# One inference step of a hybrid decoder trunk: the first layer norm split over two engines, the gate kept by channel, and new orders of work between and behind the expert products

## The chip, the cores and the metric

The kernel runs on one core of a Trainium2 chip. The time is the device time of one execution, in microseconds (us). The engines are PE (TensorE), DVE (VectorE), ACT (ScalarE), POOL (GpSimd) and SP, which here only issues DMAs. Each runs its own list of instructions in order; they meet at semaphores.

## What is computed

272 prompt tokens (16 learned ones ahead of 256) and 32 sample tokens (8 sequences of 4), 304 in all, pass through one layer of width 1024:

```python
x = layer_norm(concat(meta, x_prompt)), layer_norm(x_sample)     # ln_emb
q, fpre, vin, gate, u = split(x @ w_in + b_in)                    # five groups of 512
o = hgrn2(q, (1-lb)*sigmoid(-fpre), vin, log f)                   # 4 heads of 128
o_hg = o * rsqrt(mean(o*o) + eps) * hg_norm_g * silu(gate)
y = s5_scan(u, ...)                                               # complex diagonal scan
z = gelu(y);  o_ssm = z * sigmoid(z @ w_glu + b_glu)
x = layer_norm(ALPHA * x + concat(o_hg, o_ssm) @ w_out)           # ln1
# PEER: 8 heads, 128 x 128 product keys, top 16 of each side, then top 16
a = gelu(u_tab[e] . x);  ffn = sum(softmax(score) * a * v_tab[e])
x = layer_norm(ALPHA * x + ffn)                                   # ln2
```

The states after the last token are outputs too.

## The kernel before

All work is written out by hand, one block per engine. The 304 tokens lie in three tiles (128, 128, 48). The stages follow each other:

- First layer norm (`layer_norm`, L1067 to L1085, on DVE): statistics (L1073, L1076, L1077), subtract the mean and multiply by the gain row (L1081), ACT's square root (`deviation`, L868), reciprocal, then scale and add the bias row (L1084). The gain and bias rows are in `rows_emb`, broadcast to all partitions. PE transposes each tile (`xT`, L497), ACT copies the transposed halves into `x_t` (L885).
- Projections with fp32 matmuls: `u`, `f`, `q` in channel layout (L521; channels on partitions, 304 tokens in the row), `v` and `gate` in token layout (`project_tok`, L525 to L539). A group's weights are 2 MB in a ring of two (`load_w`, L402 to L407); group n waits for the last product of group n - 2. After `u`, SP moves u by 16 small DMAs into `u4` (L421).
- S5: DVE and POOL build its constants from `cols` and `s5raw`. POOL then makes `rot`, a chain of many small instructions that ends in `rot_ready`. PE makes `toep` and X (L578). DVE runs the scan (from L1176), after X and rot, and then reads v.
- HGRN2 in levels h = 0, 1, 2, 4, ..., 64: per level DVE makes `q_dec` (L1263), POOL `k_dec` (L1588), PE the products (L596), DVE picks them through a mask (L1229) and updates `suf` (L1273) and `pre` (L1276). Between the levels (`BETWEEN`) PE puts three gate products and then three S5 outputs `y`; DVE reads them (L1248, L1252). POOL multiplies each gate tile by its sigmoid and by the norm's gain (L1594, L1595).
- ACT runs gelu on y (L946), then makes nine masked copies of v (`v_mask`, L951). Behind them come o (L962), the transposed keys (L969), and the state products S (L679) and Sb (L684). POOL scales the sample states (L1614), DVE adds to them (L1307).
- glu; DVE scales `o_tok` and multiplies by the gate (L1313, L1315); PE transposes it (`oT`), ACT copies it (L983), PE multiplies by `w_out` (`mix`, L712, L719); second layer norm; transposes.
- PEER. Blocks of 512 KB come in by DMA. ACT rounds each half to its high part (`high_part`, L876), POOL subtracts to get the low part (L1620), PE makes three fp32r products for one fp32 one: queries (L738), expert products with u (L738; the last 48 blocks with the gate units between them, L808 and L794), and then the products with v (L835), 24 matmuls a block, which sum in 8 PSUM banks over 128 blocks. Their moving operand is `store` split into `w_hi` (ACT, L1046 and L1041) and `w_lo` (DVE, L1477, L1490, L1495), two buffers each. x1 is put together again (L1484) in eight pieces in the first v blocks.
- The ending: DVE adds the scaled x1 to the sums (L1500), PE transposes (L855), DVE makes statistics (L1507) and subtracts and multiplies (L1513), ACT scales (L1061), POOL adds the bias (L1630); for the last tile DVE does it (L1521).

The order on every engine is the order in the source. `computed` waits for a PE product, `evacuated` for its read, `link` for the instruction itself.

## Time and profile before

| | |
|---|---|
| median of 3 runs | 1229.93 us (1229.81 to 1230.38) |
| the profiled execution | 1228.41 us, its span 1226.6 us |
| instructions | 25373 |
| PE busy | 1167.3 us, 95% of the span |
| POOL busy | 848.5 us, 69% |
| DVE busy | 778.3 us, 63% |
| ACT busy | 549.3 us, 45% |
| mean granted clock of PE | 0.982 |

A row of a timeline gives the start and the duration in us (for merged instructions, of all of them), the engine, the line, the operation with what it writes and reads, how many were merged, and in brackets how long the engine had been idle and who released it. The chain that ended last is followed back from the last instruction, at each step to what released it. A granted clock of 1.00 is 2.4 GHz.

### The profile page before, as it was taken

To read this page: it belongs to the slowest core of one execution; us is meant where nothing else is said; L and a number is where in the kernel's file an instruction comes from. 1 tells how busy PE (TensorE), PEld (TensorE's weight loads), DVE (VectorE), ACT (ScalarE), POOL (GpSimd) and SP (SyncE) were. 2 spreads that over 40 slices of the span, in tenths; PEclk is the share of its full clock that TensorE was granted. 3 is DMA by queue.
4 is the path that set the end of the run, shared out by engine and by line. 5 is a ranking of instruction groups with operands and counts; after the bars stand their busy time and mean duration, and the time that the engine had idled before them with its cause. 6 is when DMAs were issued, how large, how long until landed. Compare 5 with 4: busy or idle time off the path is not lost.

```text
span 1226.6 us, 25373 instructions
## 1 busy us (share of the span) xinstructions
PE 1167.3 (95%) x8561; PEld 1103.2 (90%) x8561; DVE 778.3 (63%) x1645; ACT 549.3 (45%) x987; POOL 848.5 (69%) x745
## 2 busy tenths in 40 slices
PE   4999969989999999999999999989999999999995
PEld 3685767469899999999999999989999999999995
DVE  6908976339999999432899999953333333333336
ACT  2240132035576676776333333345554554554553
POOL 4991673056688988887555555578888888888884
PEclk9999978989999999999999999999999999999998
DMA  7331143243344445444333333344544544544442
GB/s 269 119 109 69 70 111 86 78 161 132 121 160 165 165 160 171 163 162 157 133 106 118 120 117 111 115 135 158 169 166 160 170 163 162 171 161 164 171 158 86
DMA packets 63623, 173.06 MB, mean 141 GB/s; under 512 B 9872, under 2 KB 19216, under 8 KB 63456
## 3 DMA queue, kind: packets, MB, share of 16 engines
q1 hardware_dynamic: 63584, 172.58, 42.1%
q8 instruction: 20, 0.33, 0.1%
q14 instruction: 19, 0.16, 0.0%
HBM read 167.62 MB, written 3.69 MB: 140 GB/s over the span
## 4 chain that ended last, share of the span: by engine, by line
PE 85%; DVE 9%; issue 2%; DMA 1%; SPq 1%; POOL 1%; ACT 0%; DVEq 0%; ACTq 0%; POOLq 0%
PE bank L835 33%; PE bank L738 25%; PE bank L808 13%; PE bank L794 5%; PE bank L521 3%; PE bank L712 2%; DVE q_dec L1263 2%; PE bank L694 1%; PE bank L756 1%; DVE pre L1276 1%; SPq L421 1%; DVE att L1229 1%; POOL s_samp L1614 1%; DMA w_ring<-in_w_in 1%; PE bank L563 1%
## 5 line engine op out<-in xcount | busy, mean ns | idle before, releaser
L1620 POOL TENSOR_TENSOR parts<-raw,parts 128x512 fp32r<-128x512 f32 x544 | 718.2, 1326 | 288.7 <-ACT parts L876 287.6
L876 ACT ACTIVATE parts<-raw 128x512 fp32r<-128x512 f32 x544 | 343.5, 632 | 456.9 <-PE bank L835 202.8
L835 PE MATMUL bank<-w_hi,parts 128*128 128x288 f32 x2048 | 407.6, 295 | 3.6 <-DVE w_lo L1477 2.4
L835 PEld LDWEIGHTS bank<-w_hi,parts 128*128 128x128 f32 x2048 | 327.7, 188 | 4.1 <-DVE w_lo L1477 2.6
L738 PE MATMUL bank<-xw,parts 128*128 128x288 f32 x2304 | 310.6, 296 | 2.1 <-DVE xw L1333 1.1
L738 PEld LDWEIGHTS bank<-xw,parts 128*128 128x128 f32 x2304 | 309.2, 189 | 3.2 <-issue 3.1
L835 PE MATMUL bank<-w_lo,parts 128*128 128x288 f32 x1024 | 301.5, 294 | 0.0
L1495 DVE TENSOR_TENSOR w_lo<-store,w_hi 128x288 fp32r<-128x288 f32 x122 | 147.7, 1211 | 241.5 <-ACT w_hi L1041 241.5
L835 PEld LDWEIGHTS bank<-w_lo,parts 128*128 128x128 f32 x1024 | 192.0, 188 | 0.0
L808 PE MATMUL bank<-xw,parts 128*128 128x288 f32 x1152 | 171.2, 300 | 0.0
L808 PEld LDWEIGHTS bank<-xw,parts 128*128 128x128 f32 x1152 | 156.1, 188 | 0.0
L1432 DVE TENSOR_SCALAR hot<-bank,idx_t 128x128 f32<-128x128 f32 x288 | 97.8, 401 | 0.0
L794 PE MATMUL bank<-hot 128*128 128x128 f32 x576 | 76.0, 275 | 0.0
L794 PEld LDWEIGHTS bank<-hot 128*128 128x128 f32 x576 | 71.2, 191 | 0.1
L1441 DVE TENSOR_TENSOR store<-store,bank 128x512 f32<-128x512 f32 x72 | 49.5, 688 | 24.0 <-issue 9.3
L521 PE MATMUL bank<-x_t,w_ring 128*128 128x304 f32 x192 | 53.3, 442 | 3.5 <-DMA w_ring<-in_w_in 2.9
L521 PEld LDWEIGHTS bank<-x_t,w_ring 128*128 128x128 f32 x192 | 38.5, 202 | 17.9 <-DMA w_ring<-in_w_in 3.4
L1041 ACT ACTIVATE w_hi<-store 128x288 fp32r (+1 forms) x126 | 53.9, 428 | 0.0
L1427 DVE TENSOR_TENSOR hot<-bank,idx_t 128x512 f32<-128x512 f32 x72 | 49.2, 683 | 0.2 <-DVE store L1421 0.2
L1391 DVE TENSOR_TENSOR tk_eq<-tk_eq,tk_idxf 128x512 f32<-128x512 f32 (+1 forms) x24 | 35.1, 1502 | 0.4
L1588 POOL TENSOR_TENSOR k_dec<-k_t,suf 128x512 f32<-128x512 f32 (+1 forms) x18 | 27.8, 1567 | 10.0 <-DVE suf L1273 7.6
L1357 DVE MAX8 tk_val<-scores 128x8 f32<-128x128 f32 (+1 forms) x96 | 20.9, 277 | 20.4 <-ACT scores L1003 19.6
(295 smaller groups left out, 1027.3 us busy)
## 6 DMA issues: line engine op xcount, KB each, us to landing
raw<-in_blocks SPq DMA_DIRECT2D x272, 512.0 KB, 3.2
w_ring<-in_w_in SPq DMA_DIRECT2D x5, 2048.0 KB, 8.6
w_ring<-in_w_out SPq DMA_DIRECT2D x2, 2048.0 KB, 7.8
s_samp<-in_state SPq DMA_DIRECT2D x8, 256.0 KB, 5.9
rows_ln<-in_rows SPq DMA_DIRECT2D x4, 512.0 KB, 5.0
out_hg_sample<-s_samp SPq DMA_DIRECT2D x8, 256.0 KB, 5.1
rows_emb<-in_rows SPq DMA_DIRECT2D x2, 512.0 KB, 6.1
wglu<-in_w_glu SPq DMA_DIRECT2D x1, 1024.0 KB, 5.3
```

Of the source, the lines that this page charges most:

```text
L521: last = mm(b[:, 0:NT], w[:, c, m * P:(m + 1) * P], x_t[:, c, :], start=c == 0, stop=c == DC - 1)
L738: last = mm(b[:, 0:NP], w[:, a, :], xw[:, x, c, :], start=(c == 0 and (a, x) == (0, 0)), stop=(c == DC - 1 and a == 1))
L794: last = mm(b[:, v * P:(v + 1) * P], hot[:, u % 2, 0, v, :], hot[:, u % 2, 1, v, :], start=True, stop=True)
L808: last = mm(bank[s][:, 0:NP], w[:, a, :], xw[:, x, c, :], start=(c == 0 and (a, x) == (0, 0)), stop=(c == DC - 1 and a == 1))
L835: last = mm(v_bank(c)[:, 0:NP], vv, w[:, s, :], start=first and (a, w) == (0, w_hi), stop=False, skip_group_check=True)
L876: A(parts[:, q % 4, 0, :], raw[:, s % 4, (q % 2) * 512:(q % 2 + 1) * 512], ACT.Copy).then_inc(hi_ready, 1)
L1041: A(w_hi[:, s % 2, :], store[:, bass.ds(4 * i + s, 1), :].squeeze(1), ACT.Copy).then_inc(whi_ready, 1)
L1427: V.tensor_tensor(hot[:, k % 2, 0, :, :], wide_lanes, idx_t[:, 0, UNIT * k:UNIT * k + UNIT].unsqueeze(2).broadcast_to([P, UNIT, P]), ALU.i ...
L1432: last = V.tensor_scalar(hot[:, k % 2, 1, v, :], lanes, idx_t[:, 1, t:t + 1], idx_t[:, 2, t:t + 1], ALU.is_equal, ALU.mult)
L1441: V.tensor_tensor(st, st, bank[4 + k % 3][:, :].rearrange("p (t j) -> p j t", j=NK), ALU.mult).then_inc(gate_scaled, 1)
L1495: V.tensor_tensor(w_lo[:, s, :], store[:, bass.ds(2 * i + s, 1), :].squeeze(1), w_hi[:, s, :].bitcast(F32), ALU.subtract).then_inc(wlo_rea ...
L1620: G.tensor_tensor(parts[:, q % 4, 1, :], raw[:, q // 2 % 4, (q % 2) * 512:(q % 2 + 1) * 512], parts[:, q % 4, 0, :].bitcast(F32), ALU.subt ...
```

## The change

- **First layer norm.** DVE makes only the statistics (`embed_stats`) and the shift -mean * rstd (`embed_shift`). ACT normalizes a tile in one pass (`normalize`). Gain and bias are by channel (`embt`) and go on where the transposed tile is read: half of the channels by ACT (`read_x`), half by DVE. The residual needs the same in token layout; DVE multiplies x_tok by the gain row and adds the bias row later, behind the memset of `suf`.
- **DMA order.** `rows_emb` goes behind the first two weight groups, `cols` and `s5raw` behind the first; the third weight group is issued ahead of the u4 moves; `wglu` and the states no longer wait for POOL's gate.
- **Gate.** Four products in channel layout. ACT makes the sigmoid from the bank, DVE adds the bias and multiplies by the sigmoid, POOL multiplies by the norm's gain. DVE applies it where it reads the transposed o (`oT`), which ACT did before. The y parts come one level later.
- **Between the u and the v products.** ACT makes the first two `w_hi` ahead of its last gelu; DVE makes the x1_t pieces one at a time, each followed by one `w_lo`.
- **Ending.** The last two v blocks go by halves, with the transposes of the first half ahead of the last half product; the last block's `w` has its own buffer (`w_end`). DVE makes the first half's statistics between the two halves of y_t.

```diff
-            for i in range(2):
-                sp.dma_start(rows_emb[:, i, :], rows_in[i, :].partition_broadcast(P)).then_inc(rows_sem, 16)
...
-            sp.dma_start(cols[:, :], cols_in).then_inc(cols_sem, 16)
-            sp.dma_start(s5raw[:, :, :, :].rearrange("p a b c -> p (a b c)"), s5bc).then_inc(cols_sem, 16)
...
+            sp.dma_start(ident[:, :], consts_in[:, 0:P]).then_inc(ident_sem, 16)
+            sp.dma_start(embt[:, :], cols_in[:, NCOLS:NCOLS + 2 * DC]).then_inc(embt_sem, 16)
...
             load_w(0)
+            sp.dma_start(cols[:, :], cols_in[:, 0:NCOLS]).then_inc(cols_sem, 16)
+            sp.dma_start(s5raw[:, :, :, :].rearrange("p a b c -> p (a b c)"), s5bc).then_inc(cols_sem, 16)
+            load_w(1)
...
+            for i in range(2):
+                sp.dma_start(rows_emb[:, i, :], rows_in[i, :].partition_broadcast(P)).then_inc(rows_sem, 16)
...
+            load_w(2)
             for m in range(4):
                 evacuated(sp, "u", m)
             for j in range(SC):
                 for q in range(4):
                     sp.dma_start(u4[32 * j:32 * j + 32, :, :].rearrange("p (m q) n -> p m q n", q=4)[:, :, q, :],
                                  u_chan[32 * q:32 * q + 32, :, j, :]).then_inc(u4_moved, 16)
-            for n in range(2, 7):
+            for n in range(3, 7):
                 load_w(n)
...
-            sp.wait_ge(gate_done, 3)
+            evacuated(sp, "v", 2)
...
-            v_block(NK // 2 - 1, 0)
-            v_block(NK // 2 - 1, 1, final=True)
...
+            def last_product(s, h):
+
+                pe.wait_ge(wlo_ready, NK - 1 + s)
+                pe.wait_ge(lo_ready, 8 * ROUNDS - 3 + 2 * s + h)
+                hi, lo = (w_end[:, 0, :], w_end[:, 1, :]) if s else (w_hi[:, 0, :], w_lo[:, 0, :])
+                for c in range(4 * h, 4 * h + 4):
+                    for (a, w) in ((0, hi), (0, lo), (1, hi)):
+                        vv = parts[:, 2 * s + h, a, (c % 4) * P:(c % 4 + 1) * P]
+                        last = mm(v_bank(c)[:, 0:NP], vv, w, start=False, stop=False, skip_group_check=True)
+                    if s:
+                        last.then_inc(y_full, 1)
...
+            last_product(0, 0)
+            last_product(1, 0)
+            last_product(0, 1)
+            y_transposes(0)
+            last_product(1, 1)
+            y_transposes(1)
...
+            def normalize(t):
+
+                n = TILES[t][1]
+                act.wait_ge(shift_ready, t + 1)
+                A(x_tok[:n, t, :], x_tok[:n, t, :], ACT.Identity, bias=shift[:n, t:t + 1],
+                  scale=rstd[:n, 3 + t:4 + t]).then_inc(x0_ready, 1)
+
+            def read_x(t):
+
+                t0, n = TILES[t]
+                computed(act, "xT", t, 0)
+                for c in range(4):
+                    last = A(x_t[:, c, t0:t0 + n], bank_of("xT", t, 0)[:, c * n:(c + 1) * n], ACT.Identity,
+                             bias=embt[:, DC + c:DC + c + 1], scale=embt[:, c:c + 1])
+                readout(last, "xT", t, 0)
+
             deviation(0, 0)
-            for t, (t0, n) in enumerate(TILES):
-                if t < 2:
-                    deviation(0, t + 1)
-                for i in range(2):
-                    computed(act, "xT", t, i)
-                    readout(A(x_t[:, 4 * i:4 * i + 4, t0:t0 + n],
-                              bank_of("xT", t, i)[:, 0:4 * n].rearrange("p (c n) -> p c n", n=n), ACT.Copy),
-                            "xT", t, i)
+            deviation(0, 1)
+            normalize(0)
+            deviation(0, 2)
+            normalize(1)
+            act.wait_ge(embt_sem, 16)
+            read_x(0)
+            normalize(2)
+            read_x(1)
+            read_x(2)
...
+            for m in range(HEADS):
+                computed(act, "gate", m)
+                A(gate_sig[:, m, :], bank_of("gate", m)[:, 0:NT], ACT.Sigmoid, bias=gcol[:, m:m + 1]).then_inc(gate_s, 1)
...
-            for t, (t0, n) in enumerate(TILES):
-                computed(act, "oT", t)
-                readout(A(ohg_t[:, :, t0:t0 + n], bank_of("oT", t)[:, 0:4 * n].rearrange("p (h n) -> p h n", n=n),
-                          ACT.Copy), "oT", t)
...
             act.wait_ge(gate_scaled, 3 + LATE_TURNS * UNITS)
             for s in range(2):
                 A(w_hi[:, s, :], store[:, s, :], ACT.Copy).then_inc(whi_ready, 1)
+            late_gelus(V_ROUND - 1, [3])
...
-            for s in range(2, 4):
-                high_part(ROUNDS - 1, 2 * s)
-                high_part(ROUNDS - 1, 2 * s + 1)
-                w_high(NK // 4 - 1, s)
+            high_part(ROUNDS - 1, 4)
+            high_part(ROUNDS - 1, 5)
+            w_high(NK // 4 - 1, 2)
+            A(w_end[:, 0, :], store[:, NK - 1, :], ACT.Copy).then_inc(whi_ready, 1)
+            high_part(ROUNDS - 1, 6)
+            high_part(ROUNDS - 1, 7)
...
-                layer_norm(t, rows_emb, 0, rows_sem, x0_ready)
...
+            def embed_shift(t):
+
+                n = TILES[t][1]
+                dve.wait_ge(ln_std, t + 1)
+                link(V.reciprocal(rstd[:n, 3 + t:4 + t], rstd[:n, 3 + t:4 + t]))
+                V.tensor_scalar(shift[:n, t:t + 1], mv[:n, 2 * t:2 * t + 1], rstd[:n, 3 + t:4 + t], -1.0,
+                                ALU.mult, ALU.mult).then_inc(shift_ready, 1)
+
+            embed_stats(0)
+            embed_stats(1)
+            embed_shift(0)
+            embed_stats(2)
+            embed_shift(1)
+            embed_shift(2)
+            dve.wait_ge(embt_sem, 16)
+            for t, (t0, n) in enumerate(TILES):
+                computed(dve, "xT", t, 1)
+                for c in range(4):
+                    last = V.tensor_scalar(x_t[:, 4 + c, t0:t0 + n], bank_of("xT", t, 1)[:, c * n:(c + 1) * n],
+                                           embt[:, 4 + c:5 + c], embt[:, DC + 4 + c:DC + 5 + c], ALU.mult, ALU.add)
+                readout(last, "xT", t, 1)
...
+            dve.wait_ge(rows_sem, 32)
+            for t, (t0, n) in enumerate(TILES):
+                x = x_tok[:n, t, :]
+                link(V.tensor_tensor(x, x, rows_emb[:n, 0, :], ALU.mult))
+                link(V.tensor_tensor(x, x, rows_emb[:n, 1, :], ALU.add))
...
+                    dve.wait_ge(gate_s, k + 1)
+                    last = V.scalar_tensor_tensor(gate[:, k, :], b[:, 0:NT], gcol[:, k:k + 1], gate_sig[:, k, :],
+                                                  ALU.add, ALU.mult)
...
-                V.tensor_tensor(o_tok[:n, t, :], o_tok[:n, t, :], gate[:n, t, :], ALU.mult).then_inc(og_ready, 1)
+                V.tensor_tensor(ot, ot, rms[:n, 4 * t:4 * t + 4].unsqueeze(2).broadcast_to([n, HEADS, P]),
+                                ALU.mult).then_inc(og_ready, 1)
...
+            dve.wait_ge(gate_done, HEADS)
+            for t, (t0, n) in enumerate(TILES):
+                computed(dve, "oT", t)
+                readout(V.tensor_tensor(ohg_t[:, :, t0:t0 + n],
+                                        bank_of("oT", t)[:, 0:4 * n].rearrange("p (h n) -> p h n", n=n),
+                                        gate[:, :, t0:t0 + n], ALU.mult), "oT", t)
...
             for c in range(DC):
                 V.tensor_tensor(x1_t[:, c, :], xw[:, 0, c, :].bitcast(F32), xw[:, 1, c, :].bitcast(F32),
                                 ALU.add).then_inc(x1t_ready, 1)
-                if c % 4 == 3:
-                    for s in range(2):
-                        dve.wait_ge(whi_ready, 2 * (c // 4) + s + 3)
-                        j = 2 * (c // 4) + s + 2
-                        V.tensor_tensor(w_lo[:, s, :], store[:, j, :], w_hi[:, s, :].bitcast(F32),
-                                        ALU.subtract).then_inc(wlo_ready, 1)
-            with V.Fori(3, NK // 2, 1) as i:
-                for s in range(2):
+                dve.wait_ge(whi_ready, c + 3)
+                V.tensor_tensor(w_lo[:, c % 2, :], store[:, c + 2, :], w_hi[:, c % 2, :].bitcast(F32),
+                                ALU.subtract).then_inc(wlo_ready, 1)
...
+            for i in range(2):
+                for c in range(4 * i, 4 * i + 4):
+                    dve.wait_ge(y_full, c + 1)
+                    V.scalar_tensor_tensor(y_t[:, c, :], x1_t[:, c, :], ALPHA, v_bank(c)[:, 0:NP],
+                                           ALU.mult, ALU.add).then_inc(yT_ready, 1)
+                if i == 0:
+                    for t in range(3):
+                        half_stats(t, 0)
...
+                link(half_stats(t, 1))
...
-                if h >= 16:
-                    t = {16: 0, 32: 1, 64: 2}[h]
-                    n = TILES[t][1]
-                    pool.wait_ge(gate_s, t + 1)
-                    link(G.tensor_tensor(gate[:n, t, :], gate[:n, t, :], gate_sig[:n, t, :], ALU.mult))
-                    G.tensor_tensor(gate[:n, t, :], gate[:n, t, :], rows_v[:n, 2, :], ALU.mult).then_inc(gate_done, 1)
+                if h >= 8:
+                    m = {8: 0, 16: 1, 32: 2, 64: 3}[h]
+                    evacuated(pool, "gate", m)
+                    G.tensor_scalar(gate[:, m, :], gate[:, m, :], gcol[:, HEADS + m:HEADS + m + 1], None,
+                                    ALU.mult).then_inc(gate_done, 1)
```

## Rows read from the trace of the kernel before

**Rows 1.** The page's part 4: the chain that ended last, shares by engine.

```profile
PE 85%; DVE 9%; issue 2%; DMA 1%; SPq 1%; POOL 1%; ACT 0%; DVEq 0%; ACTq 0%; POOLq 0%
```

**Rows 2.** Timeline: start, duration (us), engine, line, form, idle before; 0 to 45.

```profile
4.79 1.29 DVE L1073 BATCH_NORM_STATS2 small<-x_tok 128x6 f32<-128x512 f32 x2 [3.90 <-DMA x_tok<-in_x_prompt]
...
8.72 1.28 DVE L1081 SCALAR_TENSOR_TENSOR x_tok<-x_tok,small,rows_emb 128x1024 f32<-128x1024 f32 x1 [2.21 <-DMA rows_emb<-in_rows]
...
14.42 3.67 PE L497 MATMUL bank<-ident,x_tok 128*128 128x128 f32 x16 [14.42 <-DMA lane<-in_consts]
```

**Rows 3.** The chain that ended last in order: start, duration, what; 0 to 78.

```profile
21.91 18.62 PE bank L521 x64
...
51.75 7.97 DMA w_ring<-in_w_in
...
59.77 18.33 PE bank L521 x64
```

**Rows 4.** Stretches: busy by engine (count), granted clock, DMA share, GB/s.

```profile
40.50:56.90 16.40, 16.39 (x65) 11.82 (x63) 16.05 (x27) 3.43 (x7) 15.80 (x21) 1.00 0.41 117
...
59.80:64.00 4.20, 4.20 (x10) 2.92 (x11) 2.76 (x5) 0.00 (x0) 3.81 (x16) 0.59 1.05 392
```

**Rows 5.** Timeline, 45 to 125.

```profile
60.73 0.79 DVE L1161 COPY pre<-f_t 128x1216 f32<-128x1216 f32 x1
...
60.75 0.86 POOL L348 TENSOR_TENSOR rot<-pool_tmp 128x16 f32<-128x16 f32 x1
...
92.21 0.22 POOL L348 TENSOR_TENSOR pool_tmp<-pool_tmp 128x16 f32<-128x16 f32 x1
...
96.76 1.29 DVE L1176 TENSOR_TENSOR cm_scan<-x_s,rot 128x1088 f32<-128x1088 f32 x1 [33.96 <-ACT x_s L937]
```

**Rows 6.** Timeline of the gated-attention levels, 125 to 178.

```profile
136.73 0.69 DVE L1248 TENSOR_TENSOR gate<-bank,rows_v 128x512 f32<-128x512 f32 x1
...
155.17 2.01 POOL L1595 TENSOR_TENSOR gate<-gate,rows_v 128x512 f32<-128x512 f32 x1
...
156.09 1.65 DVE L1276 TENSOR_TENSOR pre<-pre 128x512 f32<-128x512 f32 x1
...
165.48 5.61 ACT L951 ACTIVATE v_mask<-v_tok,lane 48x512 f32<-48x512 f32 x9
...
169.80 4.08 DVE L1276 TENSOR_TENSOR pre<-pre 128x512 f32<-128x512 f32 x1
```

**Rows 7.** Timeline of the states and of the mix, 178 to 260.

```profile
179.31 1.17 PE L679 MATMUL bank<-v_tok,k_end 128*128 128x128 f32 x8
...
190.57 9.43 POOL L1614 TENSOR_TENSOR s_samp<-s_samp,pre 128x512 f32<-128x512 f32 x8 [13.12 <-PE bank L668]
...
212.72 1.31 ACT L983 ACTIVATE ohg_t<-bank 128x512 f32<-128x512 f32 x3
...
213.64 3.67 PE L712 MATMUL bank<-w_ring,ohg_t 128*128 128x512 f32 x8
```

**Rows 8.** Timeline between the expert stages, 796 to 817.

```profile
796.51 0.69 DVE L1441 TENSOR_TENSOR store<-store,bank 128x512 f32<-128x512 f32 x1 [0.15 <-PE bank L794]
...
800.91 0.75 ACT L1046 ACTIVATE w_hi<-store 128x288 fp32r<-128x288 f32 x2
...
802.38 0.40 PE L835 MATMUL bank<-w_hi,parts 128*128 128x288 f32 x1 [2.38 <-DVE w_lo L1477]
...
811.29 4.84 DVE L1484 TENSOR_TENSOR x_t<-xw 128x288 f32<-128x288 f32 x4
...
816.63 0.40 PE L835 MATMUL bank<-w_hi,parts 128*128 128x288 f32 x1 [1.27 <-DVE w_lo L1490]
```

**Rows 9.** Timeline of the ending, from 1208.

```profile
1213.07 1.29 DVE L1507 BATCH_NORM_STATS2 small<-bank 128x6 f32<-128x512 f32 x2 [1.36 <-PE bank L855]
...
1216.34 1.15 ACT L1061 ACTIVATE y_tok<-y_tok,small 128x1024 f32<-128x1024 f32 x1 [1.31 <-DVE small L1518]
...
1224.15 0.34 SPq L478 DMA_DIRECT2D out_y_sample<-y_tok  x1
```

More of the change, by code:

```diff
@@ L513, in weights, with project_part @@
                 return w_ring[:, n % 2, :, :]
+            def project_part(kind, m):
+                w = weights(W_GROUP[kind])
+                b = begin(kind, m)
+                for c in range(DC):
+                    last = mm(b[:, 0:NT], w[:, c, m * P:(m + 1) * P], x_t[:, c, :],
+                              start=c == 0, stop=c == DC - 1)
+                last.then_inc(ps_full, 1)
             def project(kind):
[L517 removed]
                 for m in range(4):
[L519 to L523 removed]
+                    project_part(kind, m)
             def project_tok(kind, t):
@@ L1030, in _, with late_gelus @@
                 u_blocks(i)
-            with act.Fori(U_ROUND + EARLY // 4, V_ROUND, 1) as i:
-                for s in range(4):
+            def late_gelus(i, slots):
+                for s in slots:
                     high_part(i, 2 * s + 4)
```

129 lines of the change are left out of this document (67 added, 62 removed).

## The prediction

> **What bounds the kernel now.** Read the chain of work that ended last first: TensorE carries 85% of it and the vector engine 9% [rows 1]. So an edit is worth time where the chain is not on TensorE, or where TensorE waits. Five such places are touched. (1) The start: the first layer norm waits 2.21 us for its gain and bias rows and then passes over each tile twice [rows 2]; TensorE starts the projections at 21.91, waits until 59.77 for the third group of weights, and needs 18.33 us for the third group against 16.4 for the second [rows 3, 4]. (2) From 96.76 the chain is on the vector engine (the S5 scan, then the gated-attention levels), whose first instruction there had waited 33.96 us [rows 5]. (3) The levels and the state products behind them [rows 6, 7]. (4) Two waits between and in the expert stages, 2.38 and 1.27 us [rows 8]. (5) The ending after the last product [rows 9]. Everything between these is TensorE back to back and is not changed.
>
> **The start.** x_tok's first tile is there at 4.79 [rows 2]. The rows are no longer ahead of tile 1: 1 MB less in the queue, so I take tile 1 at 6.8 (estimate: 0.5 MB behind a tile that landed at 4.79, at the 392 GB/s that the queue moves in the last row of [rows 4]). Statistics cost 1.29 for two halves [the same form in rows 2, 9] plus some 0.35 for the two small instructions behind them (estimate), so tile 0's end at 6.4, tile 1's at 8.5, the shift at 8.8. ACT then normalizes a tile in 1.15, the price of its 128x1024 pass with a scale [rows 9]: tile 0 10.0, tile 1 12.0, and, behind four reads of tile 0, tile 2 14.2. TensorE's transposes take 1.8 per tile at the rate of the row of 14.42 (16 in 3.67 [rows 2]). The bank reads become four of 128x128 per half tile: at least 0.5 (one wide read, a third of the 1.31 in [rows 7] and a little more), at most 4 x 0.69 (four of the wide bank read of DVE [rows 6]); I take 1.1 on ACT and 1.4 on DVE, between them, since each is a quarter as wide. The last ends at 16.4. Weights group 0 has 1.3 MB ahead of it instead of 3.1 and lands near 13 (estimate by the same rate), so it doesn't bind. The u projection starts at 16.5 instead of 21.91: -5.4, between -4 and -6. Next, group 2's load is issued ahead of the 16 small u4 moves instead of behind them. It can go when u is done (35.1), needs the 7.97 of [rows 3] and is there at 43; f ends at 51.5. The wait (56.9 to 59.8) goes, and with it the slow first stretch of q: the granted clock was 0.59 for 4.2 us after that wait, towards the lower of the two levels (1.2 GHz), and q took 18.33 where f took 16.4. So q ends at 67.8 instead of 78.1, -10.3, and X, behind it on TensorE and read by ACT, 10.3 earlier as well: about 86.0.
>
> What is late next? The scan also waits for rot, a chain of small GpSimd instructions that ends at 92.43 [rows 5]. It hangs on the S5 constants, which ACT and DVE begin after the x reads: it moves by only -5.5, to 86.9. And the change puts six new vector instructions beside it: x_tok times gain, plus bias, for three tiles, directly behind the suf memset, at about 55 to 64, with both inputs in SBUF. Each is nearly the 128x1088 form of 1.29 [rows 5]: 1.2, so 7.3 together. They fall on the middle of GpSimd's chain. Rows 5 show what that does: while DVE copied 128x1216 for 0.79 us, GpSimd's 16-column instruction lasted 0.86 against 0.22 for its like at 92.21, so about 0.64 of 0.79 was lost. At that share (0.8) six cost 0.8 x 7.3 = 5.9, at full 7.3, at none 0; I take 6.2, a little over the share because these instructions have two SBUF inputs, while the copy had one. Rot is then ready at 93.1 and the scan starts there: **-3.6** instead of the -10 that TensorE won. Bounds -9.9 (no loss) and -2.5.
>
> The Trainium skill (SBUF — State Buffer, "Who interferes with whom") says that a vector instruction with two SBUF inputs and a GpSimd instruction that reads SBUF exclude each other for the whole instruction. By that rule alone the loss would be 7.3 and the sum 1.1 us later than mine, 1219.9; it speaks against this placement.
>
> ACT's Identity behind Sqrt does not occur in this trace; if it needed its own table the start would pay some table loads, which the rot bound would hand on. The Trainium skill (ScalarE: Activation LUTs, "Table sets: the hidden batching unit") puts identity into every set, so no load; this leaves the sum unchanged.
>
> **The levels and the states.** These are vector-bound, one level in 6.85 us (half of 156.09 to 169.80, [rows 6]). The gate is read in four channel tiles of 304 columns by one instruction instead of 512-column adds at 0.69 [rows 6]: about 0.43 each (scaled), against 0.69 twice and 0.85: -0.5. Its new wait is for ACT's sigmoid of the same bank, done about 0.5 after TensorE's product, 4.1 us of work begun a level earlier; ahead of the wait nothing else is due, behind it are q_dec and TensorE's next products. I cost it at nothing; cover 3 us. GpSimd's two 128x512 products per tile (1.7 to 2.0) leave, and one scaling of 304 columns per head comes (about 1.0). That is worth more on the vector engine than on GpSimd: the pre update of 128x512 took 1.65 beside such a product and 4.08 at the last level, queued behind the product and two of GpSimd's own k_dec [rows 6], where 512 columns alone should take about 0.68 (1.29 for 1088 columns, [rows 5]). With GpSimd idle when suf is ready, pre goes first: -0.95 twice and -3.4 once. The last level ends near -5.8 + 0.5 for the y part that now comes after it: y2 moved one level later, because four gates stand ahead of the y parts. Here the gain meets a new bound: ACT can start y2's gelu only then (pre ends at 167.6 on the old clock, read and gelu 0.5 each, estimated from the 0.69 row: 168.6), and v_mask, 5.61 for nine [rows 6], now follows at 168.6 to 174.2 instead of 165.48 to 171.1. Behind v_mask stand on ACT the read of o and of the first kend, 0.5 to 0.6 each (two of the wide copies in the 1.31 of [rows 7]); the first state product starts at 175.4 instead of 179.31: **-3.9**, between -2 (a late y2 product) and -5.3 (ACT not binding). From there the chain is as now: states, the second and third o, GpSimd's s_samp (9.43 from 190.57 [rows 7]), glu. The weight load for glu, the state loads and the 16 z moves on SP no longer stand behind the gate product on GpSimd; they are hidden already and gain nothing. keysT goes behind the outputs, 60 us before its use.
>
> The gate now multiplies in channel layout on the read of oT, on DVE instead of ACT. The vector engine saves three products, hidden by its wait for ACT's last glu sigmoid. But its 0.69 read can start only behind the last ossm product (about 213.53), where ACT's copy of 212.72 ran beside it and TensorE went on at 213.64 [rows 7]: 214.3, **+0.65**, between 0 and 0.8.
>
> **The seam.** TensorE waits 2.38 before 802.38 for w_lo, which came behind ACT's last gelu: w_hi started at 800.91 [rows 8]. The gate scaling on which w_hi depends is done at 797.2 (0.69 from 796.51, [rows 8]), so in the new order w_hi is made near 797.8 to 798.5 and w_lo near 799.3; the ACT work pushed back (two high parts, the last gelu) moves by 0.1, and the vector engine's last two late products are due only at the seventh and eighth bank of the block, 2.4 us in. Gain 2.38. The second wait, 1.27 before 816.63, is that of four x1_t sums in one piece, 4.84 under GpSimd's products, ahead of w_lo [rows 8]; one at a time (1.2) plus a w_lo (1.3) is 2.5 per block of 3.2. Gain 1.27. **-3.65**, between -2.4 and -3.7.
>
> **The ending.** Twelve transposes (1.4) go ahead of the last half product, so that ends 1.4 later. DVE has read half 0 of three tiles by then, but these three 0.65 push the last y_t to about 1213.5, transposes to 1214.1, and statistics start at 1214.2 instead of 1213.07. Each of the three tiles then takes 0.65 less than the 3.15 of now (1213.07 to 1216.34 less ACT's start [rows 9]): +1.1 - 1.95 = -0.8 for the sample tile, whose store is issued at 1224.15; the second prompt tile, through ACT and GpSimd, gains only some 0.2. **-0.6**, between +0.5 and -1.3.
>
> **Sum.** -3.6 - 3.9 + 0.65 - 3.65 - 0.6 = -11.1. The profiled execution took 1228.41 with a span of 1226.6, and the median is 1229.93, 0.12% off; so the span would be 1215.5, and the median **1218.8**.
>
> **Rivals.** (A) GpSimd's chain is not slowed, or only little: the scan starts at 86.9 and the whole start gain comes, 1212.5. For it: GpSimd's instructions are short and have their own overhead to hide in. Against it: the 0.86 row. Chance 0.2, with what lies between (1213 to 1216) 0.1 more. (B) The attention gain is swallowed, since y2's product or ACT's v_mask comes later than I think, or the seam keeps its wait because w_lo meets GpSimd's product: each alone costs 3.65 to 3.9, 1222.5 to 1222.7. For it: y2 is a chain of three engines in the one place where all are busy. Chance 0.12. (C) Slower than before: TensorE idles some 10 us before level 1, since its projections are early and the scan is not, and stays at the lower clock in the levels. There 24 products of 128x128 at 0.229 and 16 of 304 columns at 0.51 (twice 16.4/64) make 13.7 a level against the vector engine's 6.85, so 6.85 lost a level; it decides against the change from two whole levels (13.7), and four give 1246. Against it: after the wait before 59.77 the clock was back within 4.2 us of matmuls [rows 4]. Chance 0.03. (D) The change doesn't do what it says, each place being hidden by another: within 0.2%, chance 0.02; against it, five separate waits.
>
> **How the numbers follow.** The forecast and its neighbours from 1216 to 1222 hold 0.53, A with its partial form 0.3, B 0.12, C 0.03, D 0.02. The range reaches from 1211.5, A with a little more at the end, to 1223, B: about 0.85. 0.2% (2.5 us) is what a measurement can tell from no change. Faster 0.95, same 0.02, slower 0.03.
>
> **What would show it.** Profile after: first projection near 16.5 with no wait at the third group; the last rot instruction at about 93 and the scan's first instruction released by GpSimd, not by ACT's X read (A: near 87, released by either); the last pre update at 0.7; v_mask starting right after a gelu, with ACT not idle ahead of kend; no wait over 0.3 on TensorE between 795 and the end. Wrong if rot's end moves with the u projection, if a level lasts over 7 us, or if TensorE waits for the banks that DVE's late products free.

## The result and the profile after

The changed kernel takes 1224.09 us in the median of five executions (1220.96 to 1224.97) against 1229.93: a ratio of 0.9953, 95% interval 0.9940 to 0.9965, 5.8 us faster. In a second comparison the same two took 1221.14 and 1228.9 (0.9936, 0.9919 to 0.9952), 7.8 us. The ratios are formed on their own and differ a little from those of the medians; where two comparisons are set against each other below, both are given. 1218.8 had been forecast, 11.1 faster. The profiled execution took 1220.96, with a span of 1219.2 against 1226.6: 7.4 less. So two things are to be explained: 3.7 us missing from the profiled execution, and up to 4 us by which other executions of the changed kernel are longer than the profiled one.

The chain that ended last, shares by engine: less of it is on the vector engine than in [rows 1].

```profile
PE 90%; DVE 5%; issue 2%; POOL 1%; ACT 1%; DMA 0%; SPq 0%; DVEq 0%; POOLq 0%
```

The start answers [rows 2, 3, 5]. Columns of a timeline as there; 4 to 95 us, and the chain's piece of the projections first.

```profile
17.14 51.86 PE bank L530 x192
```

```profile
4.91 1.29 DVE L1139 BATCH_NORM_STATS2 small<-x_tok 128x6 f32<-128x512 f32 x2 [4.04 <-DMA x_tok<-in_x_prompt]
...
9.99 3.79 PE L507 MATMUL bank<-ident,x_tok 128*128 128x128 f32 x16 [9.99 <-ACT x_tok L909]
...
57.96 1.23 DVE L1243 TENSOR_TENSOR x_tok<-x_tok,rows_emb 128x1024 f32<-128x1024 f32 x1
...
58.13 1.16 POOL L354 TENSOR_TENSOR pool_tmp<-rot,pool_tmp 128x32 f32<-128x32 f32 x1
59.25 1.30 POOL L355 TENSOR_TENSOR pool_tmp<-rot,pool_tmp 128x32 f32<-128x32 f32 x1
...
77.53 0.25 POOL L354 TENSOR_TENSOR pool_tmp<-rot,pool_tmp 128x32 f32<-128x32 f32 x1
...
86.59 0.74 ACT L980 ACTIVATE x_s<-bank 128x456 f32<-128x456 f32 x2 [0.79 <-PE bank L591]
...
93.44 0.22 POOL L359 TENSOR_TENSOR pool_tmp<-pool_tmp 128x16 f32<-128x16 f32 x1
...
94.04 1.29 DVE L1257 TENSOR_TENSOR cm_scan<-x_s,rot 128x1088 f32<-128x1088 f32 x1 [28.58 <-PE bank L552]
```

The projections run in one piece from 17.14 (21.91 before), without the wait for the third group, and end at 69.00 instead of 78.10. The scan starts only 2.7 us earlier, and what it waits for has changed. Before, rot was complete at 92.43 and the scan stood 4.3 us behind it, released by ScalarE's read of X ([rows 5]). Now ScalarE has read X at 87.33, and the scan begins 0.4 us behind GpSimd's last rot instruction (93.44 plus 0.22); the profile's naming of TensorE as the releaser doesn't fit these times.

The levels and the states, ScalarE's and TensorE's rows; they answer [rows 6, 7]. Here o(t) is the attention output of tile t, and the state product is the first of S, the prompt's state.

```profile
166.28 0.46 ACT L990 ACTIVATE z<-z 128x304 f32<-128x304 f32 x1 [5.18 <-DVE z L1329]
166.64 5.61 ACT L995 ACTIVATE v_mask<-v_tok,lane 48x512 f32<-48x512 f32 x9
172.16 0.57 ACT L1006 ACTIVATE o_tok<-bank 128x512 f32<-128x512 f32 x1
172.63 1.54 ACT L1013 ACTIVATE k_end<-bank 128x512 f32<-128x512 f32 x3
173.26 2.08 PE L692 MATMUL bank<-v_tok,k_end 128*128 128x128 f32 x8 [2.67 <-ACT k_end L1013]
...
176.73 0.63 PE L669 MATMUL bank<-s_prompt,q_dec 128*128 128x128 f32 x2
...
181.79 0.42 PE L675 MATMUL bank<-v_tok,att 48*48 48x128 f32 x4 [1.26 <-issue]
...
186.87 9.43 POOL L1709 TENSOR_TENSOR s_samp<-s_samp,pre 128x512 f32<-128x512 f32 x8 [15.68 <-PE bank L681]
```

The same place in the kernel before: a pair of o(1), the start of o(2), and then two stretches behind 178: busy time by engine, granted clock, DMA share, GB/s.

```profile
181.61 0.39 PE L656 MATMUL bank<-s_prompt,q_dec 128*128 128x128 f32 x2
...
185.49 0.42 PE L662 MATMUL bank<-v_tok,att 48*48 48x128 f32 x4 [1.26 <-issue]
```

```profile
178.00:180.00 2.00, 2.00 (x14) 1.80 (x13) 0.00 (x0) 1.55 (x3) 0.00 (x0) 0.61 1.22 290
180.00:182.00 2.00, 1.17 (x11) 1.01 (x10) 0.69 (x1) 0.15 (x1) 0.00 (x0) 1.00 1.21 290
```

v_mask follows its gelu at once, as forecast, and the first state product waits for what ScalarE does behind it. This product starts 6.05 us earlier than in [rows 7], but its eight parts take 2.08 instead of 1.17, and the pairs of o(1) 0.63 instead of 0.39. o(2) starts at 181.79 instead of 185.49, only 3.70 earlier; GpSimd's s_samp, behind o(2), also starts 3.70 earlier: 1.0 more than the scan gave.

The mix and the ending; they answer [rows 7, 9].

```profile
210.42 1.13 PE L725 MATMUL bank<-w_ring,ohg_t 128*128 128x512 f32 x2 [0.64 <-DVE ohg_t L1403]
```

```profile
1206.80 0.70 DVE L1592 BATCH_NORM_STATS2 small<-bank 128x6 f32<-128x512 f32 x1 [0.82 <-PE bank L874]
...
1216.69 0.34 SPq L488 DMA_DIRECT2D out_y_sample<-y_tok  x1
```

Between 780 and the end TensorE now has one wait, where [rows 8] has two (2.38 and 1.27). Waits of TensorE there: line waited for, us in total, times, longest.

```profile
PE bank L874 <- DVE y_t L1597: 1.0, 1, 1.0
```

This wait is new, in the ending, where the transposes of the second half wait for y_t. The forecast's sign of "no wait over 0.3" is not met there, though its own account of the ending has the transposes behind the last y_t.

### The profile page after: what moved, and what is told of

Its sections match the earlier page's. It is cut to its first block, busy times and chain, and to the rows that moved or that the text cites. A ratio compares the mean times of both kernels' runs of the same rounds, so it can differ in the third digit from the quotient of the medians.

```text
span 1219.2 us, 25381 instructions
## 1 busy us (share of the span) xinstructions
PE 1164.7 (96%) x8561; PEld 1104.6 (91%) x8561; DVE 775.2 (64%) x1660; ACT 552.2 (45%) x994; POOL 853.2 (70%) x743
## 4 chain that ended last, share of the span: by engine, by line
PE 90%; DVE 5%; issue 2%; POOL 1%; ACT 1%; DMA 0%; SPq 0%; DVEq 0%; POOLq 0%
PE bank L845 33%; PE bank L751 25%; PE bank L821 13%; PE bank L530 5%; PE bank L807 5%; PE bank L725 2%; PE bank L609 1%; PE bank L707 1%; PE bank L769 1%; POOL s_samp L1709 1%; PE bank L591 1%; PE bank L576 1%; PE bank L732 1%; PE bank L552 1%; DVE q_dec L1340 0%
## 5 line engine op out<-in xcount | busy, mean ns | idle before, releaser
L845 PE MATMUL bank<-w_hi,parts 128*128 128x288 f32 x2016 | 400.8, 295 | 0.0
L845 PEld LDWEIGHTS bank<-w_hi,parts 128*128 128x128 f32 x2016 | 322.6, 188 | 0.0
L845 PE MATMUL bank<-w_lo,parts 128*128 128x288 f32 x1008 | 296.8, 294 | 0.0
L1574 DVE TENSOR_TENSOR w_lo<-store,w_hi 128x288 fp32r<-128x288 f32 x116 | 140.5, 1211 | 228.4 <-ACT w_hi L1084 228.4
L845 PEld LDWEIGHTS bank<-w_lo,parts 128*128 128x128 f32 x1008 | 189.1, 188 | 0.0
L530 PE MATMUL bank<-x_t,w_ring 128*128 128x304 f32 x256 | 69.3, 432 | 1.7 <-ACT x_t L917 1.7
L530 PEld LDWEIGHTS bank<-x_t,w_ring 128*128 128x128 f32 x256 | 49.8, 196 | 19.2 <-issue 3.4
L1438 DVE MAX8 tk_val<-scores 128x8 f32<-128x128 f32 (+1 forms) x96 | 20.9, 277 | 20.2 <-ACT scores L1042 19.4
```

Of the source, the lines that this page charges most:

```text
L530: last = mm(b[:, 0:NT], w[:, c, m * P:(m + 1) * P], x_t[:, c, :], start=c == 0, stop=c == DC - 1)
L845: last = mm(v_bank(c)[:, 0:NP], vv, w[:, s, :], start=first and (a, w) == (0, w_hi), stop=False, skip_group_check=True)
L1574: V.tensor_tensor(w_lo[:, s, :], store[:, bass.ds(2 * i + s, 1), :].squeeze(1), w_hi[:, s, :].bitcast(F32), ALU.subtract).then_inc(wlo_rea ...
```

## The experiments

Two theories and their rivals stand behind them. Clock: TensorE's granted clock falls to the lower level (1.2 GHz) at waits, and behind the levels that takes back what ScalarE's order leaves. Lock: the six vector products on x_tok hold GpSimd up and set the scan. The rivals: the parts themselves brought less, or the experts lost it.

**The changed kernel again.** No edit.

> The changed kernel unchanged, to see where its ordinary run (1224 us, mean granted clock 0.977) differs from the profiled one (1221.0, 0.982). Theory 1, the clock: TensorE idles longer ahead of the first state product than before, and in ordinary runs it spends about 6 us more at the lower level (1.2 GHz) somewhere between the attention levels and the first expert product, which costs about 3 us: 1224 again, and a profile at 0.977 shows such a stretch between 165 and 265 us. Theory 2, the experts: the 3 us sit in the expert stages (more waits, or slower transfers), so the stretch from the first product behind the seam to the end is longer than in the profile at hand, with the granted clock 1.00 there.

Measured: 1221.14 in the median of four (1220.03 to 1225.37); the profiled execution is the long one, 1225.37 with the granted clock at 0.976, 4.4 us above that of the first profile. Its rows:

```profile
7.74 1.29 DVE L1139 BATCH_NORM_STATS2 small<-x_tok 128x6 f32<-128x512 f32 x2 [0.96 <-DMA x_tok<-in_x_prompt]
...
189.31 11.51 PE L697 MATMUL bank<-v_mask,k_end 48*128 48x128 f32 x64
...
200.75 3.91 PE L707 MATMUL bank<-z_t,wglu 128*128 128x304 f32 x7
```

Two stretches of either profile follow, the one at hand first, then that of the first profile: busy time by engine, granted clock, DMA share, GB/s.

```profile
190.00:196.00 6.00, 6.00 (x39) 6.00 (x38) 5.72 (x10) 0.55 (x2) 6.00 (x6) 0.66 0.00 0
196.00:204.00 8.00, 8.00 (x30) 6.76 (x30) 6.02 (x11) 1.46 (x2) 1.91 (x2) 0.50 0.28 80
```

```profile
190.00:196.00 6.00, 6.00 (x42) 6.00 (x42) 4.11 (x7) 1.50 (x2) 6.00 (x5) 0.74 0.00 0
196.00:204.00 8.00, 7.68 (x19) 5.30 (x19) 7.52 (x14) 0.51 (x1) 0.30 (x1) 0.56 0.81 221
```

The 4.4 us come in four pieces, all ahead of 280 us. The second tile of x arrives at 7.74, and the vector engine, in whose row its statistics stand ahead of the first tile's shift, waits 0.96 for it; this reaches the scan (95.25 against 94.04, +1.2). From there to o(2) +0.4. The per-sample state products take 11.51 instead of 9.15, since the stretch at the lower level begins in them earlier and lasts longer, and glu waits for them, not for GpSimd: glu starts at 200.75 against 197.17, another +2.0; from there to the first expert product 0.4 comes back. The first 120 expert products take 18.98 instead of 17.79, +1.2. The experts behind are the same to 0.1 us. So the first theory's place held, and 3.2 of the 4.4 us are of the size that it gave; 1.2 are the load's arrival, which no theory had. Its forecast that the median would be 1224 again did not: three of the four executions took 1220.0 to 1221.3, where four of the first five had taken 1223.8 to 1225.0.

**The new start alone**, on the kernel before:

```diff
-                layer_norm(t, rows_emb, 0, rows_sem, x0_ready)
+            embed_stats(0)
+            embed_stats(1)
+            embed_shift(0)
...
+                link(V.tensor_tensor(x, x, rows_emb[:n, 0, :], ALU.mult))
+                link(V.tensor_tensor(x, x, rows_emb[:n, 1, :], ALU.add))
```

> The kernel before with only the new start: the two-engine layer norm, the new order of the loads, the x_t reads with gain and bias, and the six vector products on x_tok. Nothing of the levels, the seam or the ending. Theory 1: the scan starts 2.7 us earlier and everything behind it too, so 1227.2; in ordinary runs up to 3 us are given back to the clock (1228 to 1230). Rival: additive parts, 1227.2 in every run. If the products on x_tok did not slow GpSimd's chain, the scan would start at about 88 and the time would be near 1221.

Measured: 1226.58 (ten executions, 1225.28 to 1228.28) against 1228.9, ratio 0.9983 (0.9973 to 0.9992): 2.3 us, and the scan at 93.94. That is the rival's case, 2.7 us expected: what the scan gained arrives, and the clock took nothing that can be measured here.

**The new seam and the new ending alone**, on the kernel before:

```diff
+            late_gelus(V_ROUND - 1, [3])
...
-                if c % 4 == 3:
...
+            last_product(0, 1)
+            y_transposes(0)
+            last_product(1, 1)
+            y_transposes(1)
```

> The kernel before with only the new seam and the new ending. Theory 1 (the 3 us that are missing in ordinary runs of the changed kernel are the clock's, ahead of the experts): the whole 4.25 of the profile arrive in every run, 1225.7. Theory 2 (they are lost in the experts): 1227 to 1229.

Measured: 1224.72 (seven executions) against 1228.9, ratio 0.9966 (0.9954 to 0.9977): 4.2 us. Forecast for the two were 3.65 + 0.6. They arrive in full; nothing is missing in the experts.

**The channel-layout gate alone**, on the kernel before (the parts of levels, states and mix):

```diff
-        BETWEEN = {h: job for h, job in zip(LEVELS, [("gate", t) for t in range(3)] + [("y", b) for b in range(3)])}
+        BETWEEN = {h: job for h, job in zip(LEVELS, [("gate", m) for m in range(HEADS)] + [("y", b) for b in range(3)])}
```

> The kernel before with only the channel-layout gate: gate products and reads by channel, the y parts one level later, the gate's multiplication on the read of oT. Nothing of the start, the seam or the ending. Theory 1 (the forecast's step, corrected): the levels end 5.0 earlier, v_mask and the reads behind it let the first state product start 3.3 earlier, TensorE is then at the lower level for S and o(1) and only some 1.0 is left at o(2), and 0.5 goes at the mix: -0.5, between 0 and -1.5, so 1228.4 against 1228.9 for the kernel before. Rival: the step was right and the loss in the profile was chance: -3.25, 1225.6.

Measured: 1231.51 (ten executions, 1226.67 to 1233.11) against 1229.67; the ratio is 1.0007 (0.9995 to 1.0019), no difference that is clear of the noise. By the medians it is 1.8 us slower: four executions took 1226.67 to 1229.67, the other six 1231.19 to 1233.11. The 0.5 us expected are not seen. In its profile the first state product starts 3.4 us earlier (175.91 against 179.31) and again takes 2.08; o(2) is 0.84 earlier and the mix 0.26. So in the profiled execution 0.3 is left of the 3.25 forecast for this part. That profile also shows something new at the seam, whose waits this kernel keeps: behind the same wait of 2.38 the clock falls.

```profile
802.00:806.00 4.00, 3.90 (x21) 3.90 (x22) 2.80 (x8) 0.63 (x1) 1.03 (x1) 0.69 0.42 135
```

In the kernel before that stretch is at 1.00. The first 48 products behind the wait take 8.16 instead of 6.64, so it costs this execution 1.5 us; whether it is what lifts the others was not looked at.

By their ratios the three parts give -2.1 - 4.2 + 0.9 = -5.4 us, by their medians -2.3 - 4.2 + 1.8 = -4.7, against -5.8 and -7.8 measured for all of them. Each part is known to 1.2 to 1.5 us, so they add within the noise; an interplay of up to 2 us is not ruled out.

**Idle products for TensorE ahead of o(0) and of the first state product**, in the changed kernel:

```diff
+                    mm(b[:, 0:P], ident[:, :], v_tok[:, 0, 0:P], start=True, stop=True)
...
+            idle_products(("o", 0), 12)
...
                     k_ends()
+                    idle_products(("S", 0), 14)
```

> The changed kernel with idle work for TensorE: 12 products of 128x128 ahead of o(0) and 14 ahead of the first state product, in banks that the next products overwrite from their start. ScalarE's order stays, so the first state product starts at 173.3 or up to 0.5 later. Theory 1 (the slow stretch behind is the clock's answer to the idle stretch): S, o(1) up to o(2) take 6.1 instead of 8.5 to 9.0 us, and the time falls by 2 to 2.9, 1218.3 to 1219.2 against 1221.2. Rival (the clock falls there for another reason, such as the products of 48 rows or the whole chip's load): 8.5 stay and the time is that of the changed kernel or up to 0.5 more.

Measured: 1219.29, ratio 0.9914 (0.9897 to 0.993) where the changed kernel has 0.9936 in the second comparison: 2.7 us by the ratios, 1.9 by the medians, with intervals that overlap. The trace is clearer. TensorE, from the last idle products on, and the stretch 172 to 180, with the same stretch of the changed kernel below:

```profile
170.81 3.29 PE L657 MATMUL bank<-v_tok,ident 128*128 128x128 f32 x28
173.94 1.06 PE L701 MATMUL bank<-v_tok,k_end 128*128 128x128 f32 x8
...
176.12 0.39 PE L677 MATMUL bank<-s_prompt,q_dec 128*128 128x128 f32 x2
```

```profile
172.00:180.00 8.00, 5.91 (x51) 5.59 (x51) 1.81 (x5) 3.16 (x7) 0.00 (x0) 1.00 0.40 92
```

```profile
172.00:180.00 8.00, 5.91 (x29) 5.64 (x30) 0.69 (x1) 2.50 (x6) 0.00 (x0) 0.57 0.45 93
```

The state product starts 0.7 later, since the idle products overran, and from it to o(2) (180.00) it is 6.06 instead of 8.53 us. Work that computes nothing took the stretch at the lower level away: the clock theory is shown for this stretch. That agrees with the Trainium skill (TensorE: Matmul & The Clock Gate, "Part 1: The HAM clock gate (the "warmup" mystery)"), which says that the array is put to half its clock once it has idled. Both waits, the one ahead of o(0) and the one ahead of the state product, were filled at once, so which of them brings the stretch is not told apart.

**The k_end copies on VectorE instead of ScalarE**, in the changed kernel:

```diff
-                computed(act, "kend", t)
...
+                computed(dve, "kend", t)
+                readout(V.tensor_copy(k_end[:n, t, :, :],
```

> The changed kernel with one move: the three copies of k_end go from ScalarE, where they stand behind the nine v_mask copies (5.61 us), to VectorE, which is idle from 168 to 175. Theory 1 (v_mask is what the first state product waits for, and the idle TensorE then runs at the lower level): the first state product starts at about 170.0 instead of 173.26; the idle stretch before it is 0.5 us instead of 2.67, so S and the first half of o(1) may also go at full rate, 2 us more. Together 3 to 5.5 us less than the changed kernel: 1219 to 1221 against 1224. Rival: the states are bound by the GpSimd chain k_dec, q_mask, s_samp, or by the loads of s_samp, and the gain is under 1 us.

Measured: 1215.91 (1215.67 to 1216.24), ratio 0.9897 (0.9881 to 0.9914): 5.2 us less than the changed kernel beside it (4.8 by the ratios).

```profile
167.10 2.04 PE L667 MATMUL bank<-v_tok,att 128*128 128x128 f32 x8 [2.75 <-DVE att L1311]
...
170.04 1.89 DVE L1360 COPY k_end<-bank 128x512 f32<-128x512 f32 x3 [1.86 <-PE bank L646]
170.89 1.06 PE L692 MATMUL bank<-v_tok,k_end 128*128 128x128 f32 x8
```

The state product starts 2.4 earlier and goes at full rate, as do o(1) and S; o(2) is 4.8 earlier, half of it by the clock. The low level has not gone from here: in this execution it falls on o(0) (2.04 instead of 1.13) and the transposes, where TensorE would wait for GpSimd's k_dec anyway. That may be the execution and not the move, since the changed kernel's long execution has o(0) at 2.05 too.

**The products on x_tok moved to the mix**, in the changed kernel; the load of their two rows moves with them, behind those of the next layer norm:

```diff
-                link(V.tensor_tensor(x, x, rows_emb[:n, 0, :], ALU.mult))
...
+            scale_x(0)
+            scale_x(1)
...
+                    if (t, i) == (0, 1):
+                        scale_x(2)
```

> The changed kernel with the six vector products on x_tok (gain and bias of the first layer norm) moved from beside GpSimd's rot chain to the vector engine's idle time behind the reads of oT, 211 to 224 us, where GpSimd does nothing; their two rows are loaded behind those of the next layer norm. Theory 1 (two busy vector inputs hold GpSimd up): rot's last instruction at 87.3 instead of 93.44, the scan starts at 88.2, released by ScalarE's X read or by GpSimd, 5.9 earlier, and all behind it: 1215.3 against some 1221.2 for the changed kernel. Rival 1 (the six products cost GpSimd little, its chain was only shifted): under 1 us. Rival 2: the chain gains 5.9 at the scan but TensorE's clock or the loads for glu take part of it back: 1217 to 1219.

Measured: 1215.68, ratio 0.9881 (0.9864 to 0.9897), 5.5 us below the changed kernel's 1221.14 (6.8 by the ratios).

```profile
87.44 0.22 POOL L360 TENSOR_TENSOR pool_tmp<-pool_tmp 128x16 f32<-128x16 f32 x1
88.05 1.29 DVE L1252 TENSOR_TENSOR cm_scan<-x_s,rot 128x1088 f32<-128x1088 f32 x1 [30.07 <-POOLq L1675]
```

GpSimd's chain ends 6.00 us earlier with nothing changed in it, and the scan follows. The lock theory is shown, its rival (the chain had only moved) is out; that it is the vector products and not the moved load is seen in the rows at 58.13 and 59.25, where GpSimd's instructions last as long as the vector products beside them.

**Both moves.**

> Both moves together: the products on x_tok behind the reads of oT, and the copies of k_end on VectorE. Theory 1: the two are at different places of the chain and add: 1215.9 - 5.9 = 1210.0, with the first state product at about 165.0 and the second row of o at 171. Rival: the loads that start at a fixed time (the state, the weights for glu, the z moves) become late, and 1 to 3 us stay: 1211 to 1213.

Measured: 1210.96 (1209.72 to 1215.2), ratio 0.9854 (0.9832 to 0.9876); three of the four executions lie at 1211.4 or below. The two add within 0.5 us by the medians and 1.5 by the ratios.

**Idle products ahead of the last transposes of x1**, in the changed kernel, then with both moves:

```diff
+            b = begin("x1T", 2, 0)
+            for _ in range(30):
+                mm(b[:, 0:P], ident[:, :], ident[:, :], start=True, stop=True)
```

> The changed kernel with 30 products of 128x128 for TensorE in its 5.0 us of waiting ahead of the last eight transposes of x1 (before the first expert product), in a bank that these transposes then overwrite. Theory 1 (a stretch at the lower level answers an idle stretch): the low stretch at 250 to 257 us goes, and with it about half its length in time, so 2.5 to 3.0 us: 1218.2 to 1218.7 against 1221.2 for the changed kernel. Rival: the clock is low there for another reason, 1221.2 or up to 0.5 more.

> Both moves (products on x_tok late, k_end copies on VectorE) and the 30 idle products ahead of the last transposes of x1. Theory 1: the three add: 1211.0 - 2.7 = 1208.3. Rival: 1210 to 1211, the low stretch comes all the same.

Measured: 1222.39 (ratio 0.9939) and 1210.79 (0.9849), no gain in either. The stretch went as expected, the size of one term was missed:

```profile
247.70 6.86 PE L742 MATMUL bank<-ident 128*128 128x128 f32 x60
254.50 0.70 PE L507 MATMUL bank<-ident,x_tok 48*128 48x48 f32 x8
256.33 16.22 PE L754 MATMUL bank<-xw,parts 128*128 128x288 f32 x120 [1.13 <-DVE xw L1417]
```

The low stretch at 250 is gone (16.22 for 120 products, 17.79 before). But 30 products take 6.86 us, 0.229 each, in a place of 5.0. The last transposes start at 254.50 instead of 252.00; 0.8 of that stands ahead of the mix already, so TensorE came 1.7 us late, and that is what the clock gave back. With 18 and both moves:

> Both moves and 18 idle products ahead of the last transposes of x1 instead of 30. In the trace of the kernel with 30, they took 6.86 us (0.229 each) in a place of 5.0, so TensorE reached the transposes 2 us late; 18 take 4.1. Theory: the last transposes are at 240.6 again, the low stretch behind them is gone (the first 120 products take 16.2 instead of 18.6), so 2.0 to 2.4 us less than the kernel with both moves: 1208.6 to 1209.0 against 1211.0. Rival: what is left of the idle time (0.9 us, then 1.3) is enough for the clock to fall again: 1211.

Measured: 1209.66 (five executions, 1208.0 to 1211.15), ratio 0.9841 (0.9828 to 0.9855), 19.4 us below the kernel before and the fastest here. The first 120 products take 17.63 (18.61 with both moves alone), not 16.2: a part of the low stretch stays, between 242 and 247, so the gain over both moves is 1.3 us instead of 2.0 to 2.4, and with these spreads not certain.

**The per-sample state products behind glu and the transposes of o**, with both moves and 30 idle products:

```diff
+        JOBS += [("glu", m) for m in range(4)] + [("oT", t) for t in range(3)]
         JOBS += [("Sb", b) for b in range(NB)]
-        JOBS += [("glu", m) for m in range(4)] + [("oT", t) for t in range(3)]
```

The vector engine's sums on s_samp move behind the reads of oT with them.

> As the kernel with both moves and the idle products, and with the eight per-sample state products (9.15 us) behind the glu products and the transposes of o instead of ahead of them, so that glu does not wait for GpSimd's scaling of s_samp. Theory: TensorE is busy from the last state product to the mix without a wait: mix starts at 196.0 instead of 199.0, another 2.5 to 3.3 us, 1205.2 to 1205.8; if the stretch at the lower level between 180 and 191 stays, it now falls on glu or on the per-sample products alike and nothing of it is won. Rival: the vector engine, which has the squares of o, rms, the ossm products, the reads of oT and the eight sums in one row, becomes the bound ahead of the mix, and the time is that of the kernel without this move or 1 to 2 us more.

Measured: 1210.87, ratio 0.9847, the same as without it (1210.79, 0.9849). The mix starts 1.9 us earlier, and then:

```profile
187.63 10.11 PE L710 MATMUL bank<-v_mask,k_end 48*128 48x128 f32 x64
197.67 5.90 PE L725 MATMUL bank<-w_ring,ohg_t 128*128 128x512 f32 x8
```

```profile
176.00:190.00 14.00, 13.33 (x77) 10.53 (x74) 12.18 (x24) 6.55 (x10) 9.88 (x8) 1.00 0.21 70
190.00:202.00 12.00, 12.00 (x50) 9.29 (x50) 9.56 (x14) 0.00 (x0) 0.00 (x0) 0.58 0.29 80
```

Eight products of the mix take 5.90 instead of 3.70. The stretch at the lower level has moved with the per-sample products: they start at 187.63 instead of 177.09, the clock goes down near 192 instead of 181.5, and the rest of the stretch now falls on the mix.

## Why the prediction was right or wrong, point by point

**The start: right in its mechanism, 0.9 us too good.** The projections began at 17.14 instead of the 16.5 of the forecast, since the x_t reads on ScalarE (2.61 for the last eight) took longer than the 1.1 per tile that was chosen, and the S5 constants behind them moved by 4.9 instead of 5.5. The loss of GpSimd was 6.0 where 6.2 had been taken, so rot was complete at 93.66 instead of 93.1; and the scan follows it by 0.4, which the forecast had put at nothing. The table load that it ruled out did not come: ScalarE's loads are at 0.73 and 16.80, none between the square roots and the Identity passes. Rival A is what comes only when the six products stand elsewhere: then the scan starts at 88.05. The rule by which the loss would be 7.3, that of the Trainium skill (SBUF — State Buffer, "Who interferes with whom"), is borne out by the rows, and 7.3 was still not its price: the two engines alternated. Each of six GpSimd instructions lasted as long as one vector product (1.16 to 1.30 beside 1.22 to 1.23; the same form takes 0.25 alone, at 77.53), so from 58.13 to 65.58 GpSimd lost all but the 1.4 us that its own six take without them. The loss falls short of the rule's by what GpSimd did in that time.

**The levels and the states: 2.9 of 3.9 us failed, and this is the step that made the miss.** The mechanism of the levels came as forecast: pre at 0.69 in the last three, the levels 5.0 earlier relative to the scan, v_mask behind the late gelu. One term was too good: the gate's four reads took 0.53 each, 2.1 in all against 2.2 before, a gain of 0.1 and not 0.5; the state product came 3.3 earlier beyond the scan, not 3.9. The other 2.35 us are the step that failed, "From there the chain is as now". TensorE had waited 2.67 us just before the state product (and 2.75 before o(0)), and went at the lower level through S and most of o(1): 8.53 us to o(2) instead of 6.18. The kernel before has its stretch at the lower level too, up to 179.5, but its state product starts at 179.31, at its end, and takes 1.17; the changed kernel's starts inside it. The kernel with idle products and the one with k_end on VectorE both have 6.06 there, and the gate alone, whose first state product again takes 2.08, gives nothing. The forecast knew this mechanism and priced it once, in rival C, for the wrong place: in the levels, where the clock did fall ahead of level 1 (0.62 from 121.6 to 125.5) and cost nothing, since the vector engine goes from one instruction to the next there without a wait. The forecast's sign of a level over 7 us could not tell anything: the first levels last 7.03, 7.02 and 6.88 us, and 7.04, 7.03 and 7.00 in the kernel before. Behind the levels, where TensorE is the chain, it was not asked.

**The mix: 0.5 lost where 0.65 was forecast. The seam: right.** Both waits are gone. **The ending: 0.6 as forecast, but partly by luck.** The statistics start 0.6 us late against the products ahead of them (forecast 1.1), and each of the three tiles takes 0.6 less, as forecast; but the last vector instruction of the sample tile takes 2.15 instead of 1.55, beside GpSimd's addition, which the forecast did not have. The two errors cancel, and the store of the sample tile is 0.6 early.

**The sum.** -2.7 - 1.0 + 0.5 - 3.65 - 0.6 = -7.45, against 7.4 in the profiled execution. **The step from there to the median failed too**: the forecast carried over the 0.12% by which the profiled execution of the kernel before lies under its median. That kernel's 50 executions lie between 1227.3 and 1231.5, the changed kernel's nine between 1220.0 and 1225.4. The one long execution that was profiled shows what can lengthen it: it has the stretches at the lower level longer in the three places behind the levels, and a first layer norm that waits for the second tile's load. That the other long executions are long for the same reason is not shown: their mean clocks are 0.976 to 0.979, but two of the short ones have 0.979 as well. What decides in which execution the stretches are long was not found. Nor is it settled why the first comparison gave 5.8 and the second 7.8; their intervals overlap.

## What to carry to other kernels

When a part ahead of TensorE gets shorter and another engine's row doesn't, ask what TensorE does in the gap and what it runs just behind it: here a wait of 2.7 us in front of dependent products was followed by 2.4 us lost to the lower clock. Then look at which copies or reads can move to an engine that idles in that gap; one such move (three copies) brought 5.2 us, nearly as much as the whole change in its first median (5.8). A vector product with two inputs in SBUF held GpSimd up for nearly its whole length (1.0 of 1.2 us each, six times), so its place is where GpSimd has nothing to do, not merely where the vector engine has time.

## What the runs showed of the hardware

In one place the granted clock fell although TensorE waited for nothing. In the changed kernel it goes down just before 193, with TensorE busy throughout, some 5 us into the 64 per-sample products, whose operands have 48 rows and which began at 187.70. In the kernel before, these begin at 191.40 and the clock goes down near 196.7; with them moved 10 us later (the last experiment), it goes down 10 us later. So it does not fall behind waits alone. That it is the 48 rows was not tried.

A gap filled with products kept the clock up, but it had to be nearly full: with 0.93 and 1.46 us left of it, a part of the stretch stayed (17.63 us for the 120 products, 16.22 with the gap full). And the same wait of 2.38 us at the seam left the clock at 1.00 in one kernel and took it down in another (0.69 over 4 us).
